# Three-part fp32r products replaced by single plain fp32 products, on one core of Trainium2

## The reference

```python
# first block, layers i = 0 and 1; a context stream of 256 tokens goes with it
mod_l = silu(c) @ ada_w[i] + ada_b[i]              # 6 x 1024 shifts, scales, gates
a_l = rms_norm(h, norm_mix[i]) * (1 + sc1_l) + sh1_l
y_l, y_c = mixer(a_l, a_c)                         # attention: neighbourhood (0), grouped queries (1)
h = h + g1_l * y_l
h = h + g2_l * swiglu_ffn(ada_norm(h, norm_ffn[i], sh2_l, sc2_l), w_in, w_out)   # hidden 2816
# the context stream is computed in layer 0 wholly, in layer 1 as keys and values only

# second block
proj = rms_norm_2(h) @ w_in_even                   # gated short convolution, pools of 2, 4, 8, 16
h = h + mix @ w_out_even
h = h + (silu(causal_dwconv3(x @ w_gate) + b) * (x @ w_up)) @ w_down
proj = gelu(rms_norm_2(h) @ w_in_odd)              # gating with 128 x 128 spatial weights
h = h + mix @ w_out_odd
h = h + gated_conv_ffn(...)
return rms_norm_2(h, final_norm)
```

## Time and profile before

| | before |
|---|---|
| median of 3 runs | 1551.45 us (1550.06 to 1553.72) |
| the profiled execution's own time | 1551.71 us |
| its span | 1549.8 us |
| TensorE busy | 1519.9 us, 98% of the span, 9179 matmuls |
| weight loads busy | 1266.4 us, 82% |
| VectorE busy | 939.4 us, 61% |
| ScalarE busy | 704.5 us, 45% |
| read from memory | 248.94 MB, 161 GB/s |

### The profile page before, as it was taken

One profiled execution on the slowest core, in us unless ns is written; L12 is line 12 of the kernel. 1 busy time (PEld: TensorE's weight loads), 2 busy tenths in 40 slices (PEclk: granted clock), 3 DMA queues, 4 the chain that ended last, 5 costly groups with the idle time before them and its releaser, 6 DMA issues.

```text
span 1549.8 us, 21861 instructions
## 1 busy us (share of the span) xinstructions
PE 1519.9 (98%) x9179; PEld 1266.4 (82%) x9179; DVE 939.4 (61%) x1246; ACT 704.5 (45%) x976; POOL 82.1 (5%) x116
## 2 busy tenths in 40 slices
PE   7999999999999999999999999999999999999998
PEld 5777656778888888879778888899988899988887
DVE  5422586463434333456866667678789856679973
ACT  4311475242212212235764555544556546556553
POOL 2010043000000000000010000034000000000000
PEclk9999999999999999999999999999999999999999
DMA  9765423654522332463144555665565564555652
GB/s 360 244 195 174 136 42 94 216 191 135 180 92 82 109 109 69 141 235 127 55 140 133 190 181 173 217 211 177 166 201 178 186 190 145 186 191 177 194 186 82
DMA packets 244256, 251.39 MB, mean 162 GB/s; under 512 B 17229, under 2 KB 237744, under 8 KB 244160
## 3 DMA queue, kind: packets, MB, share of 16 engines
q1 hardware_dynamic: 242624, 247.48, 49.2%
q0 software_dynamic: 928, 1.87, 0.3%
q10 hardware_dynamic: 608, 0.66, 0.1%
HBM read 248.94 MB, written 1.05 MB: 161 GB/s over the span
## 4 chain that ended last, share of the span: by engine, by line
PE 73%; DVE 14%; ACT 5%; issue 2%; POOL 2%; DMA 1%; SPq 1%; DVEq 0%; ACTq 0%; POOLq 0%
PE psum L382 71%; DVE wl L368 6%; ACT wh L361 3%; PE psum L978 2%; DVE scr L2133 1%; DVE scr L2130 1%; DVE scr L2144 1%; DVE scr L2142 1%; DVE vsum L2140 1%; POOL ptmp L1896 1%; ACT scr L2074 1%; DMA raw<-in_na_w_qkv 1%; DVE sums L1034 0%; SPq L297 0%; SPq L304 0%
## 5 line engine op out<-in xcount | busy, mean ns | idle before, releaser
L368 DVE TENSOR_TENSOR wl<-raw,wh 128x2048 fp32r<-128x2048 f32 (+1 forms) x183 | 413.4, 2261 | 254.8 <-ACT wh L361 254.5
L361 ACT ACTIVATE wh<-raw 128x2048 fp32r<-128x2048 f32 (+1 forms) x183 | 344.1, 1883 | 348.5 <-PE psum L382 341.5
L382 PE MATMUL psum<-x,wh 128*128 128x512 f32 (+1 forms) x1440 | 439.0, 364 | 0.8 <-DVE x L564 0.8
L382 PE MATMUL psum<-x,wl 128*128 128x256 f32 x1248 | 350.1, 281 | 0.0
L382 PEld LDWEIGHTS psum<-x,wh 128*128 128x128 f32 x1440 | 257.6, 188 | 46.4 <-issue 1.8
L382 PE MATMUL psum<-xh,wh 128*128 128x512 f32 (+1 forms) x688 | 259.2, 377 | 0.3 <-DVE xl L724 0.3
L382 PE MATMUL psum<-xl,wh 128*128 128x512 f32 (+1 forms) x688 | 255.1, 371 | 0.0
L382 PE MATMUL psum<-xh,wl 128*128 128x512 f32 (+1 forms) x688 | 255.1, 371 | 0.0
L382 PEld LDWEIGHTS psum<-x,wl 128*128 128x128 f32 x1248 | 236.4, 189 | 0.0
L382 PEld LDWEIGHTS psum<-xh,wh 128*128 128x128 f32 x688 | 130.0, 189 | 32.3 <-issue 4.6
L382 PEld LDWEIGHTS psum<-xh,wl 128*128 128x128 f32 x688 | 130.0, 189 | 22.5
(11 more groups left out here) (282 smaller groups left out, 2038.2 us busy)
## 6 DMA issues: line engine op xcount, KB each, us to landing
raw<-in_ffn_w_in SPq DMA_DIRECT2D x44, 1024.0 KB, 5.0
pre<-in_ada_w SPq DMA_DIRECT2D x26, 1024.0 KB, 9.9
raw<-in_ada_w SPq DMA_DIRECT2D x22, 1024.0 KB, 5.1
raw<-in_w_ffn_gate SPq DMA_DIRECT2D x22, 1024.0 KB, 5.1
raw<-in_w_ffn_up SPq DMA_DIRECT2D x22, 1024.0 KB, 5.1
raw<-in_w_ffn_down SPq DMA_DIRECT2D x19, 1024.0 KB, 4.9
raw<-in_ffn_w_out SPq DMA_DIRECT2D x16, 1024.0 KB, 5.0
raw<-in_na_w_qkv SPq DMA_DIRECT2D x10, 1024.0 KB, 6.6
```

Of the source, the lines that this page charges most:

```text
L361: act.e.activation(wh[:, c % NSPL, 0:z], raw[:, p % NRAW, 0:z], ACT.Copy).then_inc(W.hi, 1)
L368: dve.e.tensor_tensor(wl[:, c % NSPL, 0:z], raw[:, p % NRAW, 0:z], wh[:, c % NSPL, 0:z].bitcast(F32), ALU.subtract).then_inc(W.lo, 1)
L382: return pe.e.matmul(o, l, r, start=start, stop=stop, skip_group_check=shared)
```

## The change

Every three-part product becomes one matmul on plain fp32 operands. A weight chunk is multiplied where it landed in `raw`, nothing is split, and the tiles `wh`, `wl` and all low tiles go. The room is given to `raw`, which has nine slots instead of three; a load now waits until TensorE has used the chunk of nine positions before. The feed-forwards go through `group_T` with 256 columns, so that a sum lies in one bank whole; VectorE reads it there, and the copies of ScalarE and the additions go. Elementwise steps write the next operand directly. The first chunks of `qkv0`, the small loads of GpSimd and the third table of the attention's biases (`load_bias(2)`) are placed elsewhere. The pools get a padded tile, which drops GpSimd's copies.

```diff
-NRAW = 3
-NSPL = 3
+NRAW = 9
...
             for p, (kind, x) in enumerate(dma):
...
+                elif (kind, x) == ("w", first_o0 + 3):
+                    sp.wait_ge(A0.step, 2)
+                    load_bias(2)
...
-                        sp.wait_ge(W.hi, before + 1)
-                        sp.wait_ge(W.lo, before + 1)
+                        sp.wait_ge(W.used, before + 1)
...
-        def split_hi(c):
...
-            act.e.activation(wh[:, c % NSPL, 0:z], raw[:, p % NRAW, 0:z], ACT.Copy).then_inc(W.hi, 1)
-
-        def split_lo(c):
...
-            dve.e.tensor_tensor(wl[:, c % NSPL, 0:z], raw[:, p % NRAW, 0:z], wh[:, c % NSPL, 0:z].bitcast(F32),
-                                ALU.subtract).then_inc(W.lo, 1)
...
         def taken(c):
-            pe.wait_ge(W.lo, c + 1)
-            return view(wh, c % NSPL, weights[c]), view(wl, c % NSPL, weights[c])
+            p = pos["w", c]
+            pe.wait_ge(s_raw[p % NRAW], landed(p))
+            return view(raw, p % NRAW, weights[c])
...
-        def three(o, ah, al, bh, bl, start, stop, shared=False):
-            mm(o, ah, bh, start, False, shared)
-            mm(o, ah, bl, False, False, shared)
-            return mm(o, al, bh, False, stop, shared)
...
-                    last = three(o[m], h[:, k - k0, w], l[:, k - k0, w], xh[:, k, 0:n], xl[:, k, 0:n],
-                                 k == ks[0] and not (shared and m), k == ks[-1], shared)
+                    last = mm(o[m], h[:, k - k0, m * P:(m + 1) * P], x[:, k, 0:n], k == ks[0] and not (shared and m), k == ks[-1], shared)
...
-        def group_wide(o, cs, x, ready, k_outer=False):
...
-                    mm(o[m], h[:, k, w], x[:, k0 + k, :, :].rearrange("p s n -> p (s n)"), k0 + k == 0, False, True)
-                    last = mm(o[m][:, 0:T], l[:, k, w], x[:, k0 + k, 0, :], False, k0 + k == total - 1, True)
...
         def score1(i, b):
...
-            for n, (x, y) in enumerate(((qh2, kh2), (qh2, kl2), (ql2, kh2))):
-                for h in range(2):
-                    r = slice(64 * h, 64 * h + 64)
-                    last = mm(b[h][:, :], x[r, p, t * P:t * P + P], y[r, p // 2, :], n == 0, n == 2)
...
+            for h in range(2):
+                r = slice(64 * h, 64 * h + 64)
+                last = mm(b[h][:, :], q2[r, p, t * P:t * P + P], k2[r, p // 2, :], True, True)
```

More of the change, by code:

```diff
@@ L413, in tiles_tok, with group_tok @@
                 ready(k)
-                x = slice(t * P, (t + 1) * P)
-                last = three(o[t], xh[:, k, x], xl[:, k, x], h[:, k, :], l[:, k, :], k == 0 and not (k_outer and t % 2), k == KT - 1, k_outer)
-            return last
-        def group_wide(o, cs, x, ready, k_outer=False):
[L421 to L427, removed]
-                    mm(o[m], h[:, k, w], x[:, k0 + k, :, :].rearrange("p s n -> p (s n)"), k0 + k == 0, False, True)
-                    last = mm(o[m][:, 0:T], l[:, k, w], x[:, k0 + k, 0, :], False, k0 + k == total - 1, True)
[L430 to L435, removed]
+                last = mm(o[t], x[:, k, t * P:(t + 1) * P], h[:, k, :], k == 0 and not (k_outer and t % 2), k == KT - 1, k_outer)
+            return last
+        def group_tok(o, c, x, ready, k_outer=False):
+            tiles_tok(o, c, x, ready, range(len(o)), k_outer).then_inc(W.used, 1)
         def halves(b):
@@ L516, in ada_add @@
             last.then_inc(A.mod, 1)
-        N = semaphores(nc, "norm", "stat root recip spread scaled xh xl coef copy")
+        N = semaphores(nc, "norm", "stat root recip spread scaled x coef copy")
         XB = [0, 16, 32, 48]
@@ L796, in qkv0_first_pe, with part, rest_pe @@
             out_ = bank[0:2], bank[2:4]
[L798 to L807 removed]
+            def part(c, k, ms=(0, 1)):
+                w = view(raw, c, weights[c])
+                pe.wait_ge(s_part[k // 2], 32)
+                pe.wait_ge(N.x, 2 * k + 2)
+                pe.wait_ge(N.scaled, 2 * k + 2)
+                for m in ms:
+                    last = mm(out_[c][m][:, :], w[:, k, m * P:(m + 1) * P], x0[:, k, :], k == 0, k == KT - 1)
                 return last
[L810 removed]
+            for b in range(3):
                 part(0, 2 * b)
[L812 to L822 removed]
+                ada_mm(2 * b + 2)
+                ada_mm(2 * b + 3)
+                part(1, 2 * b, (0,))
+                ada_fold(b + 1)
+                part(1, 2 * b, (1,))
+                part(0, 2 * b + 1)
+                part(1, 2 * b + 1)
+            part(0, 6)
+            part(0, 7).then_inc(W.used, 1)
+            ada_pe(0)
+            part(1, 6)
+            part(1, 7).then_inc(W.used, 1)
             ada_pe(1)
+        def rest_pe():
             pe.wait_ge(L.rest, NREST)
@@ L1161, in o0_pe @@
                     pe.wait_ge(O0.res, 4 * (i - 1))
-                group_T([x[:, :] for x in b], [where[step]], xh1, xl1, TT, lambda k: pe.wait_ge(A0.o_lo, 2 * k + 2), k_outer=i == 0)
+                group_T([x[:, :] for x in b], [where[step]], x1, TT, lambda k: pe.wait_ge(A0.scaled, 2 * k + 2), k_outer=i == 0)
             border_pe(0, 1, 4, O0.sum, KT - 1)
@@ L1193, in o0_act @@
             for step in st_o0:
-                split_for(split_hi, where[step])
                 if step[1] >= 1:
@@ L1371, in qkv1_pe @@
                     pe.wait_ge(A.mod, MORE + 1)
-                group_T(halves(qbank[i]), [c_qkv1[1 + i]], xh3, xl3, T, nothing)
+                group_T(halves(qbank[i]), [c_qkv1[1 + i]], x3, T, nothing)
                 if i == 0:
@@ L1568, in attention1_pe @@
             attention_pe(C1, score1, values1, last_values_pe)
-        def attention1_pool():
-            for g in range(8):
-                attention_low_pool(C1, g)
         def attention1_act():
@@ L1600, in __init__ @@
                 self.at = downs[-1]
-                mine = (3 * self.per if wide is not None else 0, 4 * self.per, 8 if to else 0, 8 if to and to[1] is not None else 0, 12 if double else 4, 4, 4 if double else 0)
+                mine = (4 * self.per, 8 if to is not None else 0, 12 if double else 4, 4, 4 if double else 0)
                 downs.append(DN._make(a + b for a, b in zip(self.at, mine)))
@@ L1765, in ffn1_act @@
+                normed_act(3, T, 1, 1, x5, k)
+            for p in range(11):
+                act.wait_ge(W.used, where["up1", 2 * p] + 1)
+                if p >= 3:
+                    act.wait_ge(G0.g1, 22 + p - 2)
+                act.e.activation(tiles1(p)[1], ring[2 * p][:, :], ACT.Tanh, scale=0.5).then_inc(G0.tanh, 1)
             down_act(D1)
@@ L2118, in scaled @@
                 s, _ = ffn2_tile(p)
-                dve.wait_ge(FW.copy, f.at.copy + 2 * p + 1)
-                dve.e.tensor_tensor(two(s), ffn2_gate(p)[0], two(s), ALU.add).then_inc(FW.sum, 1)
+                dve.wait_ge(W.used, where[f.name, 2 * p] + 1)
                 dve.wait_ge(N.copy, 2 + f.n - 4)
-                dve.wait_ge(FW.sum, f.at.sum + p + 1)
-                dve.e.tensor_tensor(two(s), two(s), twice(rstd), ALU.mult).then_inc(FW.scaled, 1)
+                dve.e.tensor_tensor(two(s), two(ffn2_bank(2 * p)), twice(rstd), ALU.mult).then_inc(FW.scaled, 1)
             def taps(p):
@@ L2357, in dn3_act @@
         def dn3_act():
-            for i in range(9):
-                split_for(split_hi, where["dn3", i])
             sqrt_table()
@@ L2373, in dn3_dve @@
         def dn3_dve():
-            for i in range(9):
-                split_for(split_lo, where["dn3", i])
             dve.wait_ge(L.x, 32)
```

698 lines of the change are left out of this document (196 added, 502 removed).

## The result

| | before | after |
|---|---|---|
| median of this comparison, 4 runs each | 1550.93 us (1550.06 to 1553.72) | 1846.95 us (1846.79 to 1849.00) |
| ratio | | 1.191, 95% interval 1.190 to 1.193 |
| the profiled execution: own time, span | 1551.71, 1549.8 us | 1846.94, 1845.7 us |

The changed kernel is 19% slower, within 2.1 us of the forecast. The page of after: span, busy times, granted clock, chain that ended last by engine.

The account below looks back on a forecast made before the run. The prediction took TensorE's own stream to bound the kernel: 1551.7 us, plus 314 for dearer products, minus 16 for returned waits, gives 1850; with 1 us for scores, 1849 us. Range 1837 to 1861, at 69%.

Parts of the forecast that it names:

- What bounds the kernel: Whole kernel: TensorE's own stream sets the time, busy 1519.9 of 1549.8 us; the splits on VectorE and ScalarE do not.
- The price of a plain product: TensorE's stream: a plain fp32 product takes 0.430 us for 256 columns and 0.859 for 512, from four records in series.
- the bound of 0.94 from a lone product: Upper bound for a plain product by 512 columns: 1.10 us standing alone, less 0.16 us, is 0.94 us.
- The four passes: Skill's rule that true fp32 makes four passes through the array: estimated 0.427 and 0.853 us a product at 2.4 GHz.
- The scores of layer 1: Attention of layer 1: six records become four for each of 16 units, costing nothing or 1 us less.
- What the splits give back: TensorE's waits that go without splits: start 6.9, feed-forward borders 7, pools, biases and entries 2; together 16 us.
- The start: From 19.24 us to the modulation record's end at 57.6: 7.6 us is waiting, and 6.9 us comes back.
- the modulation record that the prediction names: Modulation record closing TensorE's first stretch of 32 products: ends at 57.6 us before, forecast 56.4 after.
- The borders of the feed-forwards: TensorE's waits there for `wl`, `vsum` and a sum of squares: ten, each about 0.3 us above the idle column, 7 us.
- New waits: none: Feed-forwards: VectorE's 4.8 us fits in TensorE's 13.8 us per chunk pair; nine slots give loads about eight chunks' lead.

## Why the prediction was right, and what was off

- **What bounds the kernel** held: TensorE is at 99%, and 594 us less work on the two others bought 11.4 us.
- **The price of a plain product** held. Predicted were 0.430 and 0.859 us; the distances of starts give 0.432 and 0.8585. The products grow by 317.6 us, predicted 314. The step from four records of the earlier trace rows to long streams was sound, and the bound of 0.94 from a lone product was far from it. The four passes, which the prediction takes from the Trainium skill, FP8 and Floating Point Precision, section TensorE Precision Notes, agree with the trace: 0.432 and 0.8585 us measured, 0.427 and 0.853 estimated from them. But three passes of fp32r cost more than three quarters of that (below).
- **The scores of layer 1** were put at nothing or 1 us less and cost 2.5 more; the bias rows of `odd` were not in the sum and cost 1.6. Both are products by few rows that also went from fp32r to plain.
- **"What the splits give back", 16 us,** was the mis-sized term: 26 came back. The start gave 8.0 for a predicted 6.9, and the modulation record that the prediction names ends at 56.0 us for a predicted 56.4. That is closer than the working deserves. I had read the clock as full in all slices, but a 9 there means 90% or more, and in the profiled execution of before it was at its lower level from 27.8 to 31.2 us. So some 1.6 of the 7.6 us that I called waiting were slower records (last section). The borders of the feed-forwards, put at 7, gave 13 (`o0` to `dn02`, `o1` to `dn1`, `up2` and `dn2`, `up3` and `dn3` in the table). I had counted the visible waits, ten by 0.3 us above their column, and not the smaller delays between products.
- **The reason given for that term failed.** I wrote that removing the splits frees the waits. With all splits kept the time is the same within 1.2 us. Over the whole kernel, the longer products give VectorE the time it needs, and the waits close by themselves. Taking most of the splits away is worth 11.4 us, but only beside the faster products; the two returns are nearly the same microseconds and don't add up. What the products of before had above their prices tells them apart: 27.8 us, 17.0 with short splits, 5.7 with plain products and all splits, 4.4 after. So some 11 of the 23 us hung on the splits, and the longer products closed these and the others alike.
- **"New waits: none"** held with nine slots, but the working was too easy. I reckoned about eight chunks of 6.9 us of lead. With seven slots a wait of 5.43 us appears, so the lead at the modulation chunks of layer 0 is two slots and no more.
- The errors largely cancel: 317.6 + 4.1 - 26 = 296 against 314 - 1 - 16 = 297. The price and the bound were right by their reasons; that the time came within 2.1 us is in part luck, since a return 10 us too small met a sum of products and scores 9 us too small.

No run points to a version that beats both kernels and computes the reference. Shorter splits gain 11 us, but only by leaving splits out.

## What to carry to other kernels

Find the engine whose stream bounds the kernel and price the edit there, per product, from distances between starts: 594 us of removed work on other engines was worth 11 us, and one pass more per product cost 318 by the prices. When the bounding engine gets slower, its waits for the others can close by themselves, as here, whether their work is removed or not. A size such as the number of slots can be far from its edge in most stages and two steps from it in one, so look for the stage with mixed loads, and run the kernel whose number you quote.

## What the runs showed that I had not expected

- A three-part record comes every 0.120 and 0.227 us for 256 and 512 columns, that is 0.013 above the 0.107 that 256 columns cost. A plain record, as long as two passes over them, takes 0.216 and 0.429, only 0.001 to 0.002 above 0.214 and 0.428. So four passes cost 1.20 times three (0.432 against 0.360) and 1.26 times (0.8585 against 0.680), and not 1.33.
- Plain records by 128 columns come every 0.11 us or so (11 records from 1349.83 span 1.39 us with the last one's end), with a weight load each, and still keep pace with their columns.
- In the profiled execution of before, the granted clock at the start fell to its lower level, 1.2 GHz, after TensorE had waited 0.97 and 1.50 us; in after it stayed at 2.4. Windows of before and of after:

```profile
27.50:31.00 3.50, 3.50 (x10) 2.78 (x11) 2.71 (x10) 2.07 (x4) 0.00 (x0) 0.54 1.09 386
```

```profile
19.00:31.00 12.00, 12.00 (x80) 5.46 (x82) 2.42 (x9) 1.48 (x3) 0.00 (x0) 1.00 1.09 384
```

From 27.8 to 31.2 us the records of before come 0.43 us apart instead of 0.227, which is some 1.6 us of the 8.0 that the start returned. The page's slices of 39 us don't show it. These 1.6 us are not shown to be an effect of the change. With the shorter splits TensorE waited 1.31 and 1.30 us at the same places, and in the kernel with plain wide pairs 0.90 and 1.26, and in both the clock stayed at 2.4; the start and `qkv0` took 170.0 and 169.6 us there, against 170.7.
